# A three-layer block on one core: five seams reordered, two attention sections regrouped, sixteen unread products of ones

## The reference

```python
h = rms_norm(x, g); q, k, v, p = split(h @ w_in)              # first layer
x = x + concat([attention(q, k, v), pool(p)]) @ w_out
x = x + conv_ffn(rms_norm(x, g2), w_up, conv_w, conv_b, w_down)
h = concat([meta, x])                                          # 16 + 256 tokens
z_a, xs, B, C, dt_f, dt_b, z_b, v, g = split(rmsnorm(h) @ w_even)
y_a = rmsnorm((ssd(forward) + ssd(backward) + D * xs) * silu(z_a))
y_b = silu(layernorm(conv31(v * sigmoid(g)))) * silu(z_b)
h = h + concat([y_a, y_b]) @ w_out_even
q, k, v, z = split(rmsnorm(h) @ w_odd)                         # 32 heads of 64
h = h + (neighbourhood_attention(q, k, v) * silu(z)) @ w_out_odd
return rmsnorm(h)[:, 16:]
```

## Time and profile before

| | |
|---|---|
| median of 3 runs | 2472.02 us (2472.01 to 2472.95) |
| the profiled execution | 2471.23 us |
| its span, first to last instruction | 2469.2 us |
| busy: TensorE, VectorE, ScalarE, GpSimd | 98%, 73%, 47%, 24% |
| mean granted TensorE clock | 0.998 |
| DMA | 438 MB, mean 177 GB/s |

### The profile page before, as it was taken

One profiled execution on the slowest core, in us unless ns is written; L12 is line 12 of the kernel. 1 busy time (PEld: TensorE's weight loads), 2 busy tenths in 40 slices (PEclk: granted clock), 3 DMA queues, 4 the chain that ended last, 5 costly groups with the idle time before them and its releaser, 6 DMA issues.

```text
span 2469.2 us, 54093 instructions
## 1 busy us (share of the span) xinstructions
PE 2430.7 (98%) x18918; PEld 2331.8 (94%) x18918; DVE 1791.3 (73%) x3174; ACT 1159.8 (47%) x1663; POOL 587.1 (24%) x434
## 2 busy tenths in 40 slices
PE   8999999999999999999999999999999999999997
PEld 7999899999999888889999999999999999999986
DVE  6877877777777655578888878888862666666665
ACT  5444444444444444446665733333544444444443
POOL 0400000000000000014423357777777111111100
PEclk9999999999999999999999999999999999999999
DMA  8544655555555666665555545555554554545544
GB/s 278 192 166 137 201 181 179 187 180 187 184 187 187 206 183 186 186 219 184 171 173 167 175 155 177 172 172 193 170 172 170 179 161 159 161 154 163 161 142 139
DMA packets 152249, 438.15 MB, mean 177 GB/s; under 512 B 32307, under 2 KB 47068, under 8 KB 152044
## 3 DMA queue, kind: packets, MB, share of 16 engines
q1 hardware_dynamic: 148988, 424.97, 52.0%
q0 software_dynamic: 3184, 12.14, 1.9%
HBM read 434.88 MB, written 11.09 MB: 181 GB/s over the span
## 4 chain that ended last, share of the span: by engine, by line
PE 77%; DVE 11%; issue 5%; ACT 5%; DVEq 1%; DMA 1%; POOL 1%; ACTq 0%; SPq 0%; POOLq 0%
PE bank L1091 18%; PE bank L1093 18%; PE bank L1092 18%; PE bank L1086 11%; PE bank L1087 6%; DVE wlo L1534 3%; ACT whi L623 2%; DVE c L1930 1%; PE bank L1323 1%; PE bank L1450 1%; ACT cv L796 1%; ACT cg L796 1%; PE bank L1428 1%; POOL ef L529 1%; DVE cg L1841 1%
## 5 line engine op out<-in xcount | busy, mean ns | idle before, releaser
L1091 PE MATMUL bank<-xhl,whi 128*128 128x256 f32 (+1 forms) x4492 | 1290.3, 287 | 8.2 <-DVE wlo L1534 6.4
L1093 PE MATMUL bank<-xhl,wlo 128*128 128x256 f32 (+1 forms) x4492 | 1279.5, 285 | 0.0
L1092 PE MATMUL bank<-xhl,whi 128*128 128x256 f32 (+1 forms) x4492 | 1276.9, 284 | 0.0
L623 ACT CAST whi<-raw 128x1024 fp32r<-128x1024 f32 x784 | 810.7, 1045 | 680.1 <-PE bank L1093 547.1
L1534 DVE TENSOR_TENSOR wlo<-raw,whi 128x1024 fp32r<-128x1024 f32 x624 | 765.8, 1238 | 244.9 <-ACT whi L623 241.8
L1091 PEld LDWEIGHTS bank<-xhl,whi 128*128 128x128 f32 x4492 | 847.2, 189 | 13.4 <-DVE wlo L1534 6.2
L1093 PEld LDWEIGHTS bank<-xhl,wlo 128*128 128x128 f32 x4492 | 847.7, 189 | 0.0
L1092 PEld LDWEIGHTS bank<-xhl,whi 128*128 128x128 f32 x4492 | 845.9, 188 | 0.8 <-issue 0.2
L564 POOL TENSOR_TENSOR wlo<-raw,whi 128x1024 fp32r<-128x1024 f32 x160 | 383.8, 2407 | 126.8 <-ACT whi L623 126.7
L1086 PE MATMUL bank<-fhl,whi 128*128 128x512 f32 x928 | 329.4, 399 | 1.4 <-DVE wlo L1534 1.4
L1087 PE MATMUL bank<-fhl,wlo 128*128 128x256 f32 x960 | 264.5, 281 | 0.0
(11 more groups left out here) (281 smaller groups left out, 2529.4 us busy)
## 6 DMA issues: line engine op xcount, KB each, us to landing
raw<-w_up SPq DMA_DIRECT2D x176, 512.0 KB, 4.1
raw<-w_na SPq DMA_DIRECT2D x128, 512.0 KB, 3.6
raw<-w_ssm SPq DMA_DIRECT2D x96, 512.0 KB, 3.7
raw<-w_glu SPq DMA_DIRECT2D x96, 512.0 KB, 3.5
...
```

Of the source, the lines that this page charges most:

```text
L623: A.copy(whi[s][:, :], raw[s][:, :]).then_inc(sem("hi_done"), 1)
L1091: T.matmul(out, wh, mh[:, o:o + n], start=head, stop=False)
L1092: T.matmul(out, wh, ml[:, o:o + n], start=False, stop=False)
L1093: ins = T.matmul(out, wl, mh[:, o:o + n], start=False, stop=last)
```

## The change

Nothing of what is computed is left out; sixteen products are added that nobody reads.
- Start: TensorE multiplies `ones` by `ones` sixteen times into bank 2 before it waits for the first weights.
- `pin`: the column sum goes ahead of product 3 instead of 4; ScalarE's norm goes ahead of a cast; on VectorE the variance goes ahead of the copy of the bias row, and the Newton step ahead of a `split`.
- `newton`: two TENSOR_TENSOR, one TENSOR_SCALAR, one TENSOR_TENSOR become one TENSOR_TENSOR and two SCALAR_TENSOR_TENSOR.
- Slots 1 to 7: chunk 2 runs ahead of `turning`; on VectorE `turned` moves behind `low(S, 3)`.
- `na`: `nvalues` of the pair before and the transposes of v (`nvturn`) move behind chunk 0, on both sides of `nscores`; ScalarE copies `nvr`, no longer VectorE; `pair_out`, and `pair_gate` with it, stand behind `split` 3; pair 1 stands outside the loop. The entry of `naout` follows the same scheme.
- First tiles of `naout`: the cast and the `wlo` go ahead of the squares.
- Last two tiles of `naout` and the end: the last tile is made with three matmuls of 256 columns (`wide=False`), so that VectorE adds once; the column sum is split in two accumulating products, one of `acc` ahead of the last chunk, one of the last squares; the last norm has 256 columns.

Cut to its core:

```diff
@@ -635,11 +635,11 @@
-    def norm(n):
+    def norm(n, from_=0):
...
         act.wait_ge(sem("nv_ready"), n + 1)
-        ch.link(A.activation(nt[:, :], nv[:, :], ACT.Ln))
-        A.activation(nt[:, :], nt[:, :], ACT.Exp, scale=-0.5).then_inc(sem("r0_ready"), 1)
+        ch.link(A.activation(nt[:, from_:TOK], nv[:, from_:TOK], ACT.Ln))
+        A.activation(nt[:, from_:TOK], nt[:, from_:TOK], ACT.Exp, scale=-0.5).then_inc(sem("r0_ready"), 1)
@@ -700,8 +700,8 @@
     split("pin", 1, 0)
+    norm(0)
     split("pin", 1, 1)
-    norm(0)
@@ -1018,10 +1018,19 @@
+    def nvalues_in(i):
+        act.wait_ge(sem("nvt_done"), i)
+        for n, rows in enumerate((NR, NK - NR)):
+            ins = A.copy(nvr[0:rows, :].rearrange("p (b n c) -> p b n c", b=2, n=2)[:, :, n, :],
+                         bank[2][0:rows, :].rearrange("p (b n c) -> p b n c", b=2, n=2)[:, :, n, :])
+        ins.then_inc(sem("nvr_ready"), 1)
...
                 split("na", i, j)
+            if attn and j == 0:
+                nvalues_in(i)
@@ -1037,6 +1046,7 @@
     split("naout", 0, 0)
+    nvalues_in(NPAIR)
@@ -1046,16 +1056,13 @@
     for n in range(4):
-        if n == 3:
-            split("naout", 1, 3)
+        split("naout", 1, n)
...
         gained(n // 2, n % 2)
-        if n < 3:
-            split("naout", 1, n)
...
     residual("naout", 5)
-    norm(6)
+    norm(6, META)
@@ -1069,7 +1076,8 @@
-    def product(phase, i, j, k, mh, ml, kts, width, off, n, start, stop, to=None, done=True):
+    def product(phase, i, j, k, mh, ml, kts, width, off, n, start, stop, to=None, done=True,
+                wide=True):
@@ -1080,7 +1088,7 @@
             head, last = start and n_ == 0, stop and n_ == len(kts) - 1
-            if phase in ("mix", "down", "naout"):
+            if wide and phase in ("mix", "down", "naout"):
@@ -1110,6 +1118,9 @@
+    pe.wait_ge(sem("ones_ready"), 1)
+    for n in range(16):
+        T.matmul(bank[2][:, 0:P], ones[:, :], ones[:, :], start=True, stop=True)
@@ -1131,7 +1142,7 @@
     for n in range(2, 8):
-        if n == 4:
+        if n == 3:
@@ -1333,12 +1344,12 @@
             similarity(S)
-            chunk_(2)
+        chunk_(2)
+        if begin:
...
         if not begin:
-            chunk_(2)
@@ -1440,9 +1451,9 @@
-    def nvalues(i):
-        pe.wait_ge(sem("nps_ready"), i * 2)
-        pe.wait_ge(sem("nvr_ready"), i)
+    def nvalues(i, back=0):
+        pe.wait_ge(sem("nps_ready"), i * 2 - back * 2)
+        pe.wait_ge(sem("nvr_ready"), i - back)
@@ -1452,7 +1463,14 @@
-    def na(i, attn):
+    def nvturn():
+        for b_ in range(2):
+            T.transpose(bank[2][0:NR, 2 * b_ * P:2 * b_ * P + P], nvt[:, b_ * NR:b_ * NR + NR], ident[:, :])
+            ins = T.transpose(bank[2][0:NK - NR, (2 * b_ + 1) * P:(2 * b_ + 2) * P],
+                              nvt[:, 240 + 40 * b_:296 + 40 * b_], ident[:, :])
+        ins.then_inc(sem("nvt_done"), 1)
+    def na(i, attn, more=True):
@@ -1464,21 +1482,16 @@
             if attn and j == 0:
+                if more:
+                    nvalues(i, 1)
                 nscores(i)
+                nvturn()
...
                 nturn(i)
-            if attn and j == 6:
-                nvalues(i)
-            if j == 6:
-                for b_ in range(2):
-                    T.transpose(bank[2][0:NR, 2 * b_ * P:2 * b_ * P + P], nvt[:, b_ * NR:b_ * NR + NR],
-                                ident[:, :])
-                    ins = T.transpose(bank[2][0:NK - NR, (2 * b_ + 1) * P:(2 * b_ + 2) * P],
-                                      nvt[:, 240 + 40 * b_:296 + 40 * b_], ident[:, :])
-                ins.then_inc(sem("nvt_done"), 1)
...
     na(0, False)
-    with pe.Fori(1, NPAIR) as i:
+    na(1, True, False)
+    with pe.Fori(2, NPAIR) as i:
@@ -1487,7 +1500,9 @@
     projecting(0, 0, range(8), start=True)
+    nvalues(NPAIR, 1)
     nscores(NPAIR)
+    nvturn()
@@ -1507,14 +1522,22 @@
         product("naout", 2, j, j // 2, oh, ol, ktiles(j), SEQ, 0, SEQ, j % 2 == 0, j % 2 == 1)
-    with pe.Fori(3, 8) as i:
+    def last_products(i, last=False):
...
                 pe.wait_ge(sem("bank_free"), tile("naout", i, j // 2) + 1)
+            if last and j == 3:
+                pe.wait_ge(sem("acc_done"), 2 + 95)
+                T.matmul(bank[2][:, META:TOK], ones[:, :], acc[:, META:TOK], start=True, stop=False)
             product("naout", i, j, j // 2, oh, ol, ktiles(j), SEQ, 0, SEQ, j % 2 == 0,
-                    j % 2 == 1)
-    pe.wait_ge(sem("acc_done"), 2 + 96)
-    norm(6)
+                    j % 2 == 1, wide=not last or j < 2)
+    with pe.Fori(3, 7) as i:
+        last_products(i)
+    last_products(7, last=True)
+    pe.wait_ge(sem("sq_done"), 96)
+    T.matmul(bank[2][:, META:TOK], ones[:, :], sq[:, TOK + META:2 * TOK], start=False,
+             stop=True).then_inc(sem("ss_done"), 1)
@@ -1565,24 +1588,23 @@
         ch.link(V.tensor_tensor(t, r0, r0, MUL))
-        ch.link(V.tensor_tensor(t, t, var, MUL))
-        ch.link(V.tensor_scalar(t, t, -0.5, 1.5, MUL, ADD))
-        ch.link(V.tensor_tensor(out, r0, t, MUL))
-    def norm_begin(n, e):
+        ch.link(V.scalar_tensor_tensor(out=t, in0=t, scalar=-0.5, in1=var, op0=MUL, op1=MUL))
+        ch.link(V.scalar_tensor_tensor(out=out, in0=t, scalar=1.5, in1=r0, op0=ADD, op1=MUL))
+    def norm_begin(n, e, from_=0):
...
         dve.wait_ge(sem("ss_done"), n + 1)
-        V.tensor_scalar(nv[:, :], bank[2][:, 0:TOK], 1.0 / D, e, MUL,
+        V.tensor_scalar(nv[:, from_:TOK], bank[2][:, from_:TOK], 1.0 / D, e, MUL,
...
-    def norm_end(n, out):
+    def norm_end(n, out, from_=0):
...
         dve.wait_ge(sem("r0_ready"), n + 1)
-        newton(out[:, :], nv[:, :], nt[:, :], acc[:, :])
-    def norm(n, out, e):
-        norm_begin(n, e)
-        norm_end(n, out)
+        newton(out[:, from_:TOK], nv[:, from_:TOK], nt[:, from_:TOK], acc[:, from_:TOK])
+    def norm(n, out, e, from_=0):
+        norm_begin(n, e, from_)
+        norm_end(n, out, from_)
@@ -1631,10 +1653,11 @@
     split("pin", 1, 0)
+    norm_begin(0, EPS1)
...
     V.tensor_copy(browt[0:HEADS, :], bank[6][0:HEADS, 0:384]).then_inc(sem("brow_ready"), 1)
+    norm_end(0, rs[0])
     split("pin", 1, 1)
-    norm(0, rs[0], EPS1)
@@ -1772,33 +1795,41 @@
         def finish(i, j, k, from_, ready):
+            landed(i, j, k, from_, ready)
+            add_square(k, i * 2 + (16 * ph + k))
+        def landed(i, j, k, from_, ready, halves=2):
...
             xt = tok(x, k, i, 2, off, n)
-            if phase != "outb":
+            if phase != "outb" and halves == 2:
...
                      ).then_inc(sem("xs_ready"), 1)
-            add_square(k, i * 2 + (16 * ph + k))
...
                     split(phase, i, j)
-                if j % half == half - 1:
+                if last and phase == "naout" and j == 3:
+                    landed(i, j, 1, pbank(phase, 1), i, halves=1)
+                elif j % half == half - 1:
...
         if phase == "naout":
-            finish(0, 3, 0, pbank(phase, 0), 0)
+            landed(0, 3, 0, pbank(phase, 0), 0)
             split(phase, 1, 0)
-            finish(0, 0, 1, pbank(phase, 1), 1)
+            add_square(0, 16 * ph)
+            landed(0, 0, 1, pbank(phase, 1), 1)
             split(phase, 1, 1)
-            finish(1, 1, 0, bank[2], 1)
+            add_square(1, 16 * ph + 1)
+            landed(1, 1, 0, bank[2], 1)
             split(phase, 1, 2)
+            add_square(0, 16 * ph + 2)
@@ -2015,9 +2046,9 @@
             low(S, 2)
-            turned(S)
...
             low(S, 3)
+            turned(S)
@@ -2241,11 +2272,17 @@
-    def pair_out(i):
-        dve.wait_ge(sem("npv_done"), i)
+    def pair_out(i, back=0):
+        dve.wait_ge(sem("npv_done"), i - back)
         ch.link(V.tensor_tensor(by_rows(no[:, :]), by_blocks(bank[7][:, 0:SEQ]), by_rows(nzs[:, :]), MUL))
-        o = slice((i - 1) * SEQ, i * SEQ) if isinstance(i, int) else bass.ds(i * SEQ - SEQ, SEQ)
+        n = back + 1
+        o = slice((i - n) * SEQ, (i - n + 1) * SEQ) if isinstance(i, int) else bass.ds(i * SEQ - n * SEQ, SEQ)
         both_of(no[:, :], oh[:, o], ol[:, o]).then_inc(sem("o_ready"), 1)
+    def pair_gate(i):
+        dve.wait_ge(sem("nez_ready"), i)
+        ch.link(V.scalar_tensor_tensor(out=nzs[:, :], in0=nez[:, :], scalar=1.0, in1=nz[:, :],
+                                       op0=ADD, op1=MUL))
@@ -2281,13 +2318,14 @@
         if attn:
-            nsoft_out(i, 0)
-            nsoft_out(i, 1)
+            for m in range(4):
+                nsoft_out(i, m)
         split("na", i, 3)
+        if attn and more:
+            pair_out(i, 1)
+        if attn:
+            pair_gate(i)
         scaled("na", i, 3, 1, nz[:, :], r1, SEQ, META)
-        if attn:
-            nsoft_out(i, 2)
-            nsoft_out(i, 3)
@@ -2295,38 +2333,31 @@
         split("na", i, 6)
-        if attn:
-            pair_out(i)
-        dve.wait_ge(sem("nez_ready"), i + 1)
```

(18 more changed lines are left out.)

4 lines of the change are left out of this document (2 added, 2 removed).

## The result

The changed kernel takes 2458.59 us, the median of 4 runs (2456.79 to 2459.41), against 2472.38 us for the kernel before (2472.01 to 2472.95): a ratio of 0.9946, 95% interval 0.9933 to 0.9958, or 13.8 us less. The profiled execution of the changed kernel took 2459.41 us, 11.8 us less than that of the kernel before, with a span of 2457.6 us, 11.6 us less. It was the slowest of its four, and the 2471.23 us of the kernel before lies under all four of its set, so the two traces show less than the medians do.

What follows compares the result with a forecast made beforehand. TensorE, busy 2430.7 of 2469.2 us, was taken to bound the kernel, leaving only its gaps, the end chain and small wedged products to win. Terms summed to 10.2 us, giving 2461.8 us; range 2458.8 to 2466.4.

Steps and rivals of the forecast that it cites:

- rival of the other side: Attention pairs: ScalarE's in-order queue holds chunk 4's cast behind the `nvr` copies, a new wait; 2480.1 us, chance 4%.
- gaps behind a moved seam: Anywhere an order was moved: a new TensorE gap behind it would prove the forecast wrong; no size given.
- Ones, 0: Kernel start: sixteen products of ones speed the first real products but gain nothing; bounds -0.1 to +0.5 us.
- What would show it: Start, in the profile after: products every 0.12 us from 7.8 us, wait at `wlo` L1614 from 0.9 to about 2 us.
- Column sum, -2.6: `pin`: the sum one product earlier removes TensorE's 2.60 us gap before 40.47 us; gain between 1.5 and 2.6 us.
- next in line: `pin`, once the gap is gone: weight loads, issued earlier, against the bias-table transfers; no size given.
- Newton, -0.4: Dt product stage and attention layer entry: three operations for four save 0.2 us at each; bounds 0 and 0.6.
- the eight uses per head have no such wait behind them: Newton's eight uses per head: no TensorE wait hangs on them, so the shorter step gains 0 there.
- Slots, -2.8: State-space slots: transposes behind chunk 2 no longer wait for ScalarE's SiLU; bounds 2.0 and 3.0 us.
- Pairs, -1.5: Attention pairs: three shape switches instead of four, 0.10 us less in each of 14 pairs and once at the projection.
- Entry, -2.1: Start of the last projection: cast and `wlo` ahead of squares remove three TensorE waits; bounds 1.0 and 2.2 us.
- Tail, -0.8: After the last product: fewer additions, shorter Newton and 256 columns shorten the serial chain; bounds 0.4 and 1.2 us.

Runs made afterwards that it cites:

- experiment 7: The changed kernel without the products of ones, with the transposes of v ahead of the scores in each attention pair's group; 2459.39 us, ratio 0.9953 to the kernel before.

## Why the prediction was right, and where its terms were off

The forecast was 2461.8 us and a gain of 10.2; measured were 13.8 us between medians and 11.8 between the profiled executions. No rival of the other side showed; no pair waits for ScalarE's cast. The direction of every term held, but the sizes were too small: even the highest bounds add up to only 12.7 us (the text has 12.8), and the median of 2458.59 us lies 0.2 us under the low end of the range, 2458.8. One of its own signs against it showed, too, if a small one: gaps behind a moved seam, 0.34 us at 49 us and 0.81 us at 73 us. The sizes of the terms:

- **Ones, 0.** Right where it was argued: 13.65 against 13.58 us. What would show it was wrong: the wait at `wlo` L1614 did not grow to 2 us, for the second half of the first products waits 1.10 us for `xl` on the way. That they could cost time later was not priced. In the whole change two comparisons of medians put it at 1.6 to 1.9 us, both within their intervals, and the traces show 0.7 to 1.6 us of it in the 22 to 75 us stretch, through the table's transfer; alone they cost nothing that shows. The cause of the rest stays open.
- **Column sum, -2.6.** The mechanism was right to a few tenths: the sum at 28.82, the norm's end at 32.5 us, the gap gone. The size was not: the bounds of 1.5 and 2.6 us take the printed gap for its price. The order itself is worth 3.1 to 4.6 us: 2.76 for the gap from start to start, up to 0.8 at the q/k sum behind it, and in four of six traces some 1.5 for the slower clock behind the gap, which the prediction did not have. Of this 1.94 us arrive in the recorded trace. The text named the loads' collision with the table's transfer as next in line and gave it no price; it is 1.6 us of TensorE's lead in the change, and nothing in three of four traces without the ones.
- **Newton, -0.4.** Too small: 0.3 each at the tail and at the dt product, and up to 0.5 in the head stage, which I had at 0 for lack of a wait there (single executions). The step "the eight uses per head have no such wait behind them" was wrong for the first one: TensorE does wait for the first `qkn`.
- **Slots, -2.8.** 2.56 us in the recorded trace (0.60 + 1.96), 3.9 alone by its trace, of 3.3 between medians. The earlier arrival at slot 0 was kept but brought nothing more there: that stage waits for the decay rows, and where it doesn't, it has lost the time to the clock.
- **Pairs, -1.5.** The count of hand-overs, four to three, was right, and experiment 7 confirms it. The price was not: 0.10 us is only the step on the way in (0.22 for 0.12 us), while the first matmul behind the next hand-over is late as well, 0.19 us together. 14 times that is 2.7; measured 2.52 in the stretch.
- **Entry, -2.1.** 2.85 us. The three printed gaps are 2.14 us; each stands for 0.24 us more.
- **Tail, -0.8.** 0.9 us: 1.49 from the last product to the first result, less 0.57 for the first column sum.

One error runs through three of the terms, the column sum, the slots and the entry. A printed gap of TensorE is too short, since the end of the matmul ahead of it is modelled (0.28 us long where the next could start after 0.12). Taking gaps as they stand cost about 0.2 us for each of these eight. In the pairs, too, only the first of two late starts was counted.

Of the 13.8 us between medians the two recorded executions show only 11.8: that of before is 1.2 us faster than its median, that of the change 0.8 us slower. The first fits with a clock that had not fallen behind the 2.60 us gap, where it had in four of the five other traces with that order; the prediction had only this one to read.
